# Two token mixers in front, a feed-forward behind: how the p1 tiles are dealt out around the delta rule, and on which axis the feed-forward's inner columns lie

## The reference

```python
h = rms_norm(x, norm_gain[layer]); proj = h @ w_in[layer]        # first block, per layer
q_a, k_a, v_a, z_a, q_i, ... = split(proj)                       # "p1": q_a, k_a, v_a, silu(z_a), q_i
qkv_b = silu(causal_depthwise_conv(qkv_b, conv_w[layer]))        # q, k, v of the delta rule
q_b = l2_normalize(q_b); k_b = l2_normalize(k_b)
o_b = chunked_gated_delta_rule(q_b, k_b, v_b, beta, g)           # 8 heads of 128
...
c = rms_norm_2(h, norm_ffn[i])                                   # second block, layer 0
h = h + (silu(c @ ffn_w_gate) * (c @ ffn_w_up)) @ ffn_w_down     # 1024 -> 3584 -> 1024
```

## Time and profile before

| | |
|---|---|
| median of 3 runs | 2532.65 us (2531.95 to 2541.3) |
| the profiled execution: time, span | 2537.35 us, 2535.6 us |
| busy share of PE, DVE, ACT, POOL | 98%, 26%, 19%, 5% |
| TensorE's mean granted clock | 0.987 of full speed |
| first block: layer 0, layer 1 | to about 395 us, to about 790 us |
| feed-forward: gate and up, down | 1009.5 to 1211, 1211 to 1308 us |
| experts of the second layer | about 1570 to 2495 us |

### The profile page before, as it was taken

One profiled execution on the slowest core, in us unless ns is written; L12 is line 12 of the kernel. 1 busy time (PEld: TensorE's weight loads), 2 busy tenths in 40 slices (PEclk: granted clock), 3 DMA queues, 4 the chain that ended last, 5 costly groups with the idle time before them and its releaser, 6 DMA issues.

```text
span 2535.6 us, 46713 instructions
## 1 busy us (share of the span) xinstructions
PE 2486.1 (98%) x21159; PEld 1389.1 (55%) x21159; DVE 667.6 (26%) x1386; ACT 473.7 (19%) x802; POOL 136.3 (5%) x333
## 2 busy tenths in 40 slices
PE   9999999999999999999999999999999999999999
PEld 8766557856555775444445776344444534353444
DVE  3533533434543443000013533011010101011012
ACT  1521321432322533010003442000000000000001
POOL 4011000011000310000001210000000000000000
PEclk9999999999999999999999898999999999999999
DMA  7421344422335513444336314999999999999992
GB/s 245 147 79 57 116 129 137 139 84 68 100 104 148 158 43 104 149 149 149 135 121 162 125 47 150 366 402 395 381 394 378 377 391 385 410 376 389 395 377 94
DMA packets 194428, 542.27 MB, mean 214 GB/s; under 512 B 29200, under 2 KB 61360, under 8 KB 194224
## 3 DMA queue, kind: packets, MB, share of 16 engines
q1 hardware_dynamic: 180576, 536.82, 58.2%
q10 hardware_dynamic: 13344, 1.35, 0.4%
q0 software_dynamic: 304, 1.05, 0.1%
HBM read 538.12 MB, written 1.05 MB: 213 GB/s over the span
## 4 chain that ended last, share of the span: by engine, by line
PE 93%; DVE 4%; ACT 2%; issue 1%; DMA 0%; ACTq 0%; DVEq 0%
PE psum L407 25%; PE psum L2720 23%; PE psum L2733 11%; PE psum L710 7%; PE psum L1487 5%; PE psum L2346 4%; PE psum L1669 3%; PE psum L472 2%; PE psum L2223 1%; PE psum L2778 1%; PE psum L2771 1%; PE psum L1025 1%; PE psum L1029 1%; PE psum L1015 1%; PE psum L1956 1%
## 5 line engine op out<-in xcount | busy, mean ns | idle before, releaser
L407 PE MATMUL psum<-ring,hT 128*128 128x512 f32 (+3 forms) x1568 | 665.3, 577 | 10.2 <-ACT area L829 8.7
L407 PEld LDWEIGHTS psum<-ring,hT 128*128 128x128 f32 x1568 | 290.9, 190 | 324.2 <-issue 290.7
L2720 PE MATMUL psum<-ring,mix 128*32 128x448 f32 x4608 | 438.7, 539 | 0.2 <-DVE mix L2982 0.2
L2720 PEld LDWEIGHTS psum<-ring,mix 128*32 128x32 f32 x4608 | 148.7, 110 | 282.7 <-issue 280.9
L710 PE MATMUL psum<-hT,ring 128*128 128x256 f32 x768 | 166.4, 379 | 0.0
L710 PEld LDWEIGHTS psum<-hT,ring 128*128 128x128 f32 x768 | 145.9, 190 | 20.7 <-issue 1.0
L2733 PE MATMUL psum<-area 128*32 128x256 f32 x2688 | 148.2, 379 | 0.9 <-DVE area L2973 0.9
L2720 PE MATMUL psum<-area,mix 128*32 128x448 f32 x1536 | 147.2, 539 | 0.0
L2733 PE MATMUL psum<-ring,area 128*32 128x256 f32 x2688 | 146.5, 379 | 0.0
L2971 DVE TENSOR_TENSOR area<-area,psum 128x1344 f32<-128x1344 f32 x16 | 24.6, 1535 | 457.5 <-PE psum L2720 457.5
L2733 PEld LDWEIGHTS psum<-area 128*32 128x32 f32 x2688 | 86.5, 110 | 60.6 <-issue 3.0
(11 more groups left out here) (524 smaller groups left out, 2322.1 us busy)
## 6 DMA issues: line engine op xcount, KB each, us to landing
ring<-in_w_in_dram SPq DMA_DIRECT2D x88, 1024.0 KB, 5.1
ring<-in_moe_w_gate_dram SPq DMA_DIRECT2D x96, 896.0 KB, 6.9
ring<-in_moe_w_up_dram SPq DMA_DIRECT2D x96, 896.0 KB, 7.3
area<-in_moe_w_down_dram SPq DMA_DIRECT2D x112, 512.0 KB, 5.9
ring<-in_moe_w_down_dram SPq DMA_DIRECT2D x112, 512.0 KB, 6.4
area<-in_moe_w_gate_dram SPq DMA_DIRECT2D x32, 896.0 KB, 7.4
area<-in_moe_w_up_dram SPq DMA_DIRECT2D x32, 896.0 KB, 6.6
ring<-in_w_out_dram SPq DMA_DIRECT2D x16, 1024.0 KB, 5.1
```

The lines of the kernel that those rows point to most:

```text
L407: last = nc.tensor.matmul(acc(g)[:, t, 0:d["n"]], lhs(kk, t), w[:, k, :], start=kk == 0, stop=kk == d["nk"] - 1)
L2720: last = nc.tensor.matmul(PS[32 * j:32 * j + 32, 3 * p + b, 0:PIECE].rearrange("p (m n) -> p m n", n=32), tokens(k, b), w[:, :, j, :], sta ...
```

## The change

It has two independent parts.

**Around the delta rule.** `proj1_pe` does 4 and 8 p1 steps where it did 2 and 6, so 16 steps, two whole tiles, are done before the delta rule, which weaves the remaining 32. ScalarE reads tile 0 out before the Ln of k's norm, and tile 1 ahead of the delta rule. The shared `GDN_PLAN` becomes one list for ScalarE (`GDN_OUT`) and one for VectorE (`GDN_ROPE`). No instruction is added or taken away.

**The feed-forward.** Gate and up tiles are made as the `qkv` tiles are: weights stationary, 256 tokens moving, banks 4 and 6. The 1/rms of the tokens now lies along the free axis, so TensorE spreads it over the partitions (two matmuls into `SCALES`, bank 1), ScalarE copies it to `RSTDT`, and VectorE multiplies with it. ScalarE only makes silu. The product lands in `HFT` directly: `HTOK`, the seven turns and the copies are gone, and the down product no longer waits for the last of them. `ple_turn_pe` moves between down's steps 11 and 12.

```diff
                 told[name] = told.get(name, 0) + 1
 
         BANK = {"ba": (2,), "qkv": (0, 2), "p1": (0,), "zb": (2, 0), "gate": (2, 0), "out": (2, 0), "out2": (0, 2),
-                "pg": (0, 2), "pp": (8,)}
+                "pg": (0, 2), "pp": (8,), "ffn": (4, 6)}
         TILES, LOADS = [], []
 
         def half_view(n, shape):
...
             pair(("out2", L), A["w_out_2"][L], "dve")
             if L % 2 == 0:
                 for c in range(0, FF, 512):
-                    tile(("ffn", L), A["ffn_w_gate_2"][0], c, 512, "act")
+                    tile(("ffn", L), A["ffn_w_gate_2"][0], c, 512, "dve")
                     tile(("ffn", L), A["ffn_w_up_2"][0], c, 512, "dve")
                 DOWN[L] = len(LOADS)
                 for k in range(0, FF // P, 2):
...
                 nc.tensor.matmul(PS[:, 6, c * GH:c * GH + GH], UPPER, G3[:, c, :], start=True, stop=True)
             nc.tensor.matmul(PS[:, 6, 2 * GH:3 * GH], ONES, G3[:, 0, :], start=True, stop=True)\
                 .then_inc(sem("gdn_gc"), 1)
-            for _ in range(2):
+            for _ in range(4):
                 next(p1)
             pe.wait_ge(signal("gdn_gc_out"), reached("gdn_gc_out", L + 1))
             sums(1)
-            for _ in range(6):
+            for _ in range(8):
                 next(p1)
 
         def proj1_act(s, L, p1):
...
                 s.eng.wait_ge(sem("conv_done"), 6 * L + j + 1)
                 s.do(nc.scalar.activation(Y[:, 4 * j:4 * j + 4, :], Y[:, 4 * j:4 * j + 4, :], ACT.Silu))
 
-            def rsqrt(hq, p1=None):
+            def rsqrt(hq):
 
                 if L + hq == 0:
                     s.eng.wait_ge(sem("consts_ready"), 1)
...
                 scale, eps = (float(DK), EPSK) if hq == 0 else (1.0, EPS1)
                 s.after(nc.scalar.activation((SQ, RN)[hq], banks(4, 4), ACT.Ln, bias=eps, scale=scale)
                         .then_inc(sem("gdn_logs"), 1), "gdn_logs")
-                if p1 is not None:
-                    next(p1)
                 s.after(nc.scalar.activation((SQ, RN)[hq], (SQ, RN)[hq], ACT.Exp, scale=-0.5)
                         .then_inc(sem("gdn_rsqrt"), 1), "gdn_rsqrt")
 
...
             s.do(nc.scalar.activation(EG, GC[:, 0:2 * GH], ACT.Exp))
             s.after(nc.scalar.activation(EGL, GC[:, 2 * GH:3 * GH], ACT.Exp).then_inc(signal("gdn_eg"), 1), "gdn_eg")
             next(p1)
-            rsqrt(1, p1)
             next(p1)
+            rsqrt(1)
             conv_silu(5)
+            next(p1)
+            next(p1)
 
         ROPE_TMP = [xn_t[:, 1024 + 512 * i:1536 + 512 * i] for i in range(2)]
         KI2 = xn_t[:, 0:T * P].rearrange("p (t c) -> p t c", t=T)
...
                 setup_rest_dve(s)
             unit_length(1)
             s.eng.wait_ge(signal("gdn_eg"), reached("gdn_eg", L + 1))
-            for _ in range(3):
+            for _ in range(4):
                 next(p1)
 
 
...
         def seconds(x, lv):
             return x.rearrange("p h (b two n) -> p h b two n", two=2, n=1 << lv)[:, :, :, 1, :]
 
-        GDN_UNITS = (4, 8, 9, 10, 11, 12, 13, 14, 15, 16, 17, 18, 20, 24, 25, 26, 27, 28, 29, 30, 31, 32, 33, 34, 36)
-        GDN_PLAN = (1, 2, 2, 2, 2, 3, 3, 3, 3, 4, 4, 4, 5, 6, 6, 6, 6, 7, 7, 7, 7, 8, 8, 8, 9)
+        GDN_UNITS = (4, 7, 8, 9, 10, 11, 12, 13, 14, 15, 16, 17, 20, 23, 24, 25, 26, 27, 28, 29, 30, 32, 32, 32, 32)
+        GDN_OUT = (1, 1, 2, 2, 2, 2, 3, 3, 3, 3, 4, 4, 5, 5, 6, 6, 6, 6, 7, 7, 7, 8, 8, 8, 8)
+        GDN_ROPE = (0, 0, 0, 0, 0, 1, 1, 1, 1, 2, 2, 2, 2, 3, 4, 4, 5, 6, 6, 6, 6, 7, 7, 7, 8)
 
         def gdn_pe(pe, L):
             pe.wait_ge(sem("gdn_unit"), 2 * L + 2)
...
 
 
         HFT = view(0, (FF // P) * S).rearrange("p (k s) -> p k s", s=S)
-        SGF = [view(7168 + 1024 * i, 1024).rearrange("p (t c) -> p t c", t=T) for i in range(2)]
-        HTOK = [view(9216 + 1024 * i, 1024).rearrange("p (t c) -> p t c", t=T) for i in range(2)]
+        SGF = [view(7168 + 1024 * i, 1024).rearrange("p (j s) -> p j s", j=4) for i in range(2)]
 
         def ffn_pe(pe, L, n):
             gs = group("ffn", L)
             fresh = fresh_from(n)
 
-            def turn(f):
-                pe.wait_ge(sem("gemm_out_dve"), evacuated(gs[2 * f + 1])[1])
-                if f >= 2:
-                    pe.wait_ge(sem("ffn_HT"), f - 1)
-                transposes([(lambda t, j=j: HTOK[f % 2][:, t, j * P:(j + 1) * P]) for j in range(4)], 4 + 2 * (f % 2))\
-                    .then_inc(sem("ffn_T"), 1)
+            def columns(g, first):
+                d = TILES[g]
+                gemm_begin(pe, g)
+                if first:
+                    pe.wait_ge(sem("ht_ready"), fresh + 4)
+                for h in range(2):
+                    landed(pe, d["first"] + h)
+                for j in range(4):
+                    for k in range(KD):
+                        if first and j == 0:
+                            pe.wait_ge(sem("ht_ready"), fresh + k + 1)
+                        last = nc.tensor.matmul(
+                            acc(g)[:, j // 2, (j % 2) * S:(j % 2) * S + S],
+                            half_view(d["first"] + k // 4, (4, 512))[:, k % 4, j * P:(j + 1) * P], HT[:, k, :],
+                            start=k == 0, stop=k == KD - 1)
+                        if j == 3 and k % 4 == 3:
+                            last.then_inc(sem("weights_used"), 1)
+                    if first and j == 0:
+                        rstd_ready(pe, n)
+                        for t in range(T):
+                            last = nc.tensor.matmul(SCALES[:, t * P:(t + 1) * P], bc(RSTD[:, t:t + 1], [P, P]), IDENT,
+                                                    start=True, stop=True)
+                        last.then_inc(sem("unscaled_used"), 1)
 
             for f in range(7):
-                gemm(pe, gs[2 * f], ht_lhs, None if f else fresh)
-                gemm(pe, gs[2 * f + 1], ht_lhs)
-                if f:
-                    turn(f - 1)
-            turn(6)
-            pe.wait_ge(sem("ffn_HT"), 7)
-            ple_turn_pe(pe, L, 6)
+                columns(gs[2 * f], f == 0)
+                columns(gs[2 * f + 1], False)
+
             def down(i, dh):
                 w = half_view(DOWN[L] + i, (2, D))
                 for k in range(2):
...
                                                 stop=i == 13 and k == 1)
                 return last
 
+            pe.wait_ge(sem("norm_scales_out"), DEPTH + 1)
             for i in range(12):
                 landed(pe, DOWN[L] + i)
+                if i % 2 == 0:
+                    pe.wait_ge(sem("gemm_out_dve"), evacuated(gs[i + 1])[1])
                 down(i, 0)
                 down(i, 1).then_inc(sem("weights_used"), 1)
+            pe.wait_ge(sem("gemm_out_dve"), evacuated(gs[13])[1])
+            ple_turn_pe(pe, L, 7)
             for i in (12, 13):
                 landed(pe, DOWN[L] + i)
                 last = down(i, 0)
...
         def ffn_act(s, L, n):
             gs = group("ffn", L)
 
-            def back(f):
-                s.eng.wait_ge(sem("ffn_T"), f + 1)
-                b = 4 + 2 * (f % 2)
-                s.after(nc.scalar.activation(HFT[:, 4 * f:4 * f + 4, :], banks(b, 2).rearrange("p (k s) -> p k s", k=4),
-                                            ACT.Copy).then_inc(sem("ffn_HT"), 1), "ffn_HT")
-
+            s.eng.wait_ge(sem("unscaled_used"), KD * DEPTH + 1)
+            s.after(nc.scalar.activation(RSTDT, SCALES, ACT.Copy).then_inc(sem("norm_scales_out"), 1), "norm_scales_out")
+            for f in range(7):
+                s.eng.wait_ge(sem("gemm_out_dve"), evacuated(gs[2 * f])[1])
+                s.after(nc.scalar.activation(SGF[f % 2], SGF[f % 2], ACT.Silu).then_inc(sem("ffn_gated"), 1), "ffn_gated")
+            ple_turn_act(s, L, 7)
+
+        def ffn_dve(s, L, n, gain):
+            gs = group("ffn", L)
+            scales = bc(RSTDT.unsqueeze(1), [P, 4, S])
+
+            def columns(g):
+                return acc(g).rearrange("p b (j s) -> p (b j) s", j=2)
+
+            s.eng.wait_ge(sem("norm_scales_out"), DEPTH + 1)
             for f in range(7):
                 s.eng.wait_ge(sem("weights_used"), used(TILES[gs[2 * f]]["end"] - 1))
-                if f >= 2:
-                    s.eng.wait_ge(sem("gemm_out_dve"), evacuated(gs[2 * f - 3])[1])
-                if f == 0:
-                    rstd_ready(s.eng, n)
-                for t in range(T):
-                    ins = nc.scalar.activation(SGF[f % 2][:, t, :], acc(gs[2 * f])[:, t, :], ACT.Silu, scale=RSTD[:, t:t + 1])
-                    if t < T - 1:
-                        s.do(ins)
-                    else:
-                        s.after(ins.then_inc(sem("gemm_out_act"), 1), "gemm_out_act")
-                if f >= 2:
-                    back(f - 2)
-            back(5)
-            back(6)
-            ple_turn_act(s, L, 6)
-
-        def ffn_dve(s, L, n, gain):
-            gs = group("ffn", L)
-            for f in range(7):
-                g = gs[2 * f + 1]
```

(22 more changed lines are left out.)

## The result

| | before | changed |
|---|---|---|
| median of 9 runs | 2535.4 us (2529.55 to 2541.3) | 2521.99 us (2514.82 to 2527.35) |
| ratio | | 0.994, 95% interval 0.9927 to 0.9953 |
| profiled execution: time, span | 2537.35, 2535.6 us | 2524.58, 2522.8 us |
| mean granted clock | 0.987 | 0.988 |

The change makes the kernel 0.5 to 0.7% faster. The forecast was 15.9 us off a median of 2532.65, so 2517; with nine runs the median of before is 2535.4, and the medians lie 13.4 us apart.

A forecast was written before the change was run, and what follows sets the result against it. TensorE, busy 98% of the span, was taken to bound the kernel. Feed-forward -7.2 us and delta rule -8.7 us over two layers gave -15.9 us, from a median of 2532.65 to 2517 us; range 2507 to 2529.

The forecast's parts named there:

- Passes: Gate and up: 896 passes of 256 columns take 193.4 us against 192.3 for 448 of 512, costing 1.1 us.
- spreading: Feed-forward: TensorE's four passes that spread 1/rms over the partitions add 0.45 us.
- transposes of the embedding: Down product: the embedding's transposes, 8 passes of 128 columns counted as half a turn, stay and cost 0.43 us.
- the turns and the end: Feed-forward: five gaps of 0.87 us between pairs and 4.87 us before the down product go, 9.2 us saved.
- (a): Ahead of the delta rule: tile 1's wait for its read-out goes, 1.86 us saved per layer.
- (b): Tile boundaries in the delta rule's two halves: waits of 1.17 and 1.31 us fall to 0.1 each per layer.
- (c): Delta rule's end, per layer: the 1.10 us wait before `vn` goes; waiting for VectorE's read of `o` adds 0.9.
- (d): Sparse attention's second transposes: ScalarE's copy L1407 is in time by 0.5 us, cost 0, other end 1.5.
- (B): Rival, chance 0.2: the delta rule's waits move rather than go, leaving a gain of 7.5 us, 2525 us.
- (C): Rival, chance 0.04: weight loads of 190 ns pace the new gate and up passes; at 250 ns, 2547 us.
- (D): Rival, chance 0.11: clock falls landing elsewhere in the second block's mixers shift the total some 5 us either way; unlucky, 2522.
- no wait for L829 above 0.3 us: Sign of being right: TensorE waits at most 0.3 us for ScalarE's read-out L829, before 8.7 us in 6 waits.

The follow-up runs named there:

- silu_early: The changed kernel plus a one-column silu per layer on ScalarE after the Exps of the second half's decays: 2518.39 us, ratio 0.9935.
- shifted: The changed kernel with one p1 step moved from ahead of the first inverse to behind the unit of `o`: 2517.5 us, ratio 0.9916.
- narrow128: The changed kernel with 128 tokens moving instead of 256 in gate and up, 1792 passes instead of 896: 2533.21 us in one execution.
- ffn_only: The kernel before with only the feed-forward's part of the change: 2529.78 us, ratio 0.997.
- down_early: The kernel before, its first down matmuls put ahead of the last turn and the embedding's transposes between down's steps 11 and 12: 2530.97 us, ratio 0.9977.
- sqrt_early: `shifted` plus a one-column square root per layer on ScalarE after the square of `o`: 2516.6 us, ratio 0.9921.

## Why the prediction was right, and where it was off

**Feed-forward: right, one term by luck.** Forecast -7.2, measured -7.27 in the chain. Passes +1.1 (193.4 us for 896, forecast 193.4), spreading 0.45 (0.44), transposes of the embedding 0.43 (0.44), the turns and the end 9.2. The spreading came out at 0.45 for a wrong reason. The prediction took the turn as 16 passes in 0.87 us and got 0.22 for four of them in a stream, then chose 0.45 between this and 0.71. But a transpose is one record and not two, as the text ahead of the prediction has it for every `nc.tensor.matmul`: the turn in rows 5 is x8, the embedding's transposes x4, and TensorE's count on the page rises by 396 = 448 + 4 - 7 x 8. Eight records in 0.87 us give 0.44 for four, which is what both the spreading and the embedding's transposes took. None of the waits for which I kept a price came: not for 1/rms, not for the eight blocks of `HT`, not for weights.

**Delta rule: -3.5 per layer where -4.3 was forecast.** Sign and mechanism were right, terms were sized wrongly, in opposite ways. In layer 1, by the starts of the units in TensorE's timelines, less the steps that moved (a step is 4 passes, 1.72 us):

| step | forecast | measured |
|---|---|---|
| (a) ahead of the delta rule | -1.86 | -2.13 |
| (b) boundary in the first half | -1.17 + 0.1 | -1.44 + 0.16 |
| (b) boundary in the second half | -1.31 + 0.1 | -1.58 + 1.43 |
| (c) wait before `vn` against the wait for the read of `o` | -1.10 + 0.9 | 0.0 |
| (d) second part of the transposes | 0 | 0.0 |
| sum | -4.3 | -3.5 |

The step that failed is in (b): "against a read-out with signal of 1.17. I take 0.1 for each". The read-out of tile 4 isn't like that of tile 2; it has silu's table load in front of it, and `silu_early` shows that this is nearly the whole difference, 1.28 of 1.33 us. It stood in the code: columns from `Z0` on get `ACT.Silu`. The upper end that I kept, 1.2, was for another reason, and 1.43 lies beyond it.

The other way round, each wait that went gave 0.27 us more than its idle time. Most of it is that the first block after a stop is longer: in rows 9 the 16 passes after a wait start at 142.08 and the next matmuls (L1001) at 149.14, 7.06 us later; a block in the middle of the stream takes 6.87 (27.47 / 4, rows 4). The rest, some 0.08, is that a row's idle time starts at the modelled end of the last matmul, and this lies behind the point where the next could have started. (The prediction takes such an end for a start once: the scores began at 128.51, not at 128.67.) Three such waits went in a layer, 0.8 us, and it was luck that they made up for more than half of what the table load cost.

In (c) the two nearly cancel, as forecast, and the new wait is 0.94 (forecast 0.9); `shifted` shows that one step behind `o` removes it. In (d) the copy was in time: it ended at 655.46 and the second part started at 656.14, so by 0.7 us, forecast 0.5; `shifted`, which is later there, has the wait that was named as the other end.

**Rivals.** (B), waits that move: it came about in one of the four places only, by the table load, which its reason (margins too thin for the read-out alone) didn't name. (C), the weight loads: excluded by `narrow128`; the trace of before already had it, 48 passes of 128 columns in the 5.4 us of the scores, and I hadn't used it. (D), the clock: the unchanged mixers moved the total by several us, here -0.6 and +3.0, within the 5 us that I allowed, and in the two profiles of one kernel the clock fell at different places of them. The forecast of 2517 was 5.2 us below the median. Two plain reasons give 4.5 of it: 2.75 us because nine runs put the median of before higher than three, and 1.7 us because the code gained 14.2 instead of 15.9. The rest is within what the mixers move.

Of the signs that I had named: passes at 215.8 ns, the down product without a pause, and 0.9 us before the first transposes came; "no wait for L829 above 0.3 us" did not.

## What to carry to other kernels

When a read-out is moved, look up which function it applies and which came before it on its engine: the cover must be as long as the read-out and the table load together, or the load is pulled into idle time by a function of one column. A transpose behind a matmul whose result could have been made transposed is pure loss as long as a narrower moving operand costs next to nothing; here two passes of 256 columns cost 2.4 ns more than one of 512. And a change of half a percent is read from distances between fixed marks of the chain, which repeat to 0.01 us where the granted clock stays at 1.00, rather than from whole executions, which differ by 12. Where it doesn't, look at the clock of the stretch before you compare.

## What the runs showed of the hardware that was not expected

- A stop of TensorE between p1 blocks cost 0.27 us more than the idle time that its row gives, at all three places where one went.
- A weight load of the projections is recorded at 190 to 192 ns whether the pass lasts 429, 216 or 112 ns, and it did not stretch a pass of 216 ns; at 128 columns a pass took 112, well under the recorded length of its load.
- The same code in the mixers takes 190.4 to 197.7 us from one execution to the next, at a granted clock of 0.95 to 0.91, while the feed-forward's stretch of 355.93 us repeats to 0.01 us. The mean clock doesn't give the length; a block of eight passes took 1.78 us at 1.00 and 3.31 at 0.51.
- In four of the ten profiles the clock also fell once in layer 0 of the first block, to 0.91 over 20 us: from 120 to 140 us in `ffn_only` (the window below) and `down_early`, from 240 to 260 in `narrow128` and `sqrt_early`. Between the two `qkv` marks `ffn_only` took 390.48 us and `down_early` 390.47 where before, with the same code there, took 388.77, and `narrow128` 386.99 where the changed kernel took 385.28: 1.7 us each time.

```profile
120.00:140.00 20.00, 18.37 (x75) 11.04 (x76) 9.35 (x19) 10.88 (x11) 0.00 (x0) 0.91 0.30 105
```
